# Ids from sorted keys, a split first product, 4096-byte runs and a reordered last unit in a two-layer block kernel

## The reference

```python
scores = jax.nn.sigmoid((xt @ router_w).astype(jnp.float32))
biased = (scores + router_b).reshape(T, N_GROUPS, EXPERTS_PER_GROUP)   # 4 groups of 4 experts
group_score = lax.top_k(biased, 2)[0].sum(-1)
best_group = jnp.argmax(group_score, axis=-1)
local = lax.top_k(in_group, 2)[1]                                      # 2 experts of the best group
gate = take(scores, expert_idx); gate = gate / gate.sum(-1, keepdims=True)
...
def expert_block(args):
    xi, e = args
    return (jax.nn.silu(xi @ w_gate[e]) * (xi @ w_up[e])) @ w_down[e]   # 1024 -> 256 -> 1024
...
x = layer_norm(DEEPNORM_ALPHA * x + ffn, ln2_g[layer], ln2_b[layer])
```

## Time and profile before

| | us |
|---|---|
| median of 3 runs (1299.04 to 1300.09) | 1299.23 |
| the profiled execution, its own time | 1301.88 |
| its span, first to last instruction | 1300.1 |
| PE busy (share of the span) | 1236.1 (95%) |
| DVE busy | 837.8 (64%) |
| ACT busy | 633.7 (49%) |
| queue of DMAs issued by SP, share of 16 engines | 58.4% |

### The profile page before, as it was taken

How to read it: one execution, slowest core, us unless ns; L and a number is a source line. 1 busy time by engine, 2 the same in 40 slices (tenths; PEclk the granted TensorE clock), 3 DMA queues, 4 the chain that set the end, 5 groups by cost and what they waited for, 6 DMA issues and landing times.

```text
span 1300.1 us, 17517 instructions
## 1 busy us (share of the span) xinstructions
PE 1236.1 (95%) x7044; PEld 665.3 (51%) x7048; DVE 837.8 (64%) x1060; ACT 633.7 (49%) x705; POOL 93.6 (7%) x60
## 2 busy tenths in 40 slices
PE   7999999999999999999999998999989979899996
PEld 4676565446654444656657753433345655343333
DVE  6687776988774477555567757433786676743376
ACT  4467565445553264444456634433644584343361
POOL 1000000000000014000005200011002100001100
PEclk9999999999999999999999998999999999899999
DMA  9474444655655565656652015699954600669990
GB/s 316 147 250 160 156 130 140 224 199 189 226 195 194 195 213 186 218 202 214 198 194 66 2 66 187 226 320 369 381 200 164 225 32 33 198 222 322 368 376 35
DMA packets 152812, 258.09 MB, mean 199 GB/s; under 512 B 8913, under 2 KB 81692, under 8 KB 152732
## 3 DMA queue, kind: packets, MB, share of 16 engines
q1 hardware_dynamic: 152732, 256.98, 58.4%
HBM read 255.88 MB, written 1.07 MB: 198 GB/s over the span
## 4 chain that ended last, share of the span: by engine, by line
PE 77%; DVE 8%; DMA 5%; SPq 3%; ACT 3%; issue 2%; DVEq 1%; POOL 1%; POOLq 0%; ACTq 0%
PE ps L1108 12%; PE ps L821 10%; PE ps L1375 9%; PE ps L1152 6%; PE ps L1110 6%; PE ps L802 6%; PE ps L1068 3%; PE ps L1420 3%; PE ps L839 3%; PE ps L1358 2%; DVE w_ring L2082 2%; DMA w_ring<-in_exp_w_up 2%; PE ps L1479 2%; DMA w_ring<-in_exp_w_down 2%; PE ps L1295 2%
## 5 line engine op out<-in xcount | busy, mean ns | idle before, releaser
L2082 DVE SCALAR_TENSOR_TENSOR w_ring<-w_ring,w_hi 128x2048 f16<-128x2048 f32 (+3 forms) x155 | 345.9, 2240 | 120.4 <-ACT w_hi L1636 119.6
L1636 ACT ACTIVATE w_hi<-w_ring 128x2048 f16<-128x2048 f32 (+3 forms) x155 | 285.6, 1851 | 185.8 <-PE ps L1152 50.9
L1108 PE MATMUL ps<-actT,w_hi 128*128 128x512 f16 x608 | 197.8, 379 | 0.0
L1110 PE MATMUL ps<-actT,w_ring 128*128 128x256 f16 x608 | 165.7, 273 | 0.0
L1636 ACT ACTIVATE arena<-ps 128x256 f16<-128x256 f32 (+8 forms) x97 | 66.1, 695 | 115.5 <-PE ps L1110 74.7
L802 PE MATMUL ps<-w_hi,actT 128*128 128x512 f16 (+2 forms) x384 | 111.8, 367 | 2.8 <-DVE actT L2087 2.8
L821 PE MATMUL ps<-w_hi,actT 128*128 128x512 f16 x352 | 108.4, 383 | 2.9 <-DVE w_ring L2082 2.9
L1108 PEld LDWEIGHTS ps<-actT,w_hi 128*128 128x128 f16 x608 | 59.5, 98 | 71.5
L1375 PE MATMUL ps<-arena 128*128 128x512 f16 x224 | 67.9, 396 | 7.7 <-DVE w_ring L2082 5.1
L821 PE MATMUL ps<-w_ring,actT 128*128 128x512 f16 x192 | 73.4, 382 | 0.0
L802 PE MATMUL ps<-w_ring,actT 128*128 128x512 f16 (+2 forms) x192 | 70.5, 367 | 0.0
(11 more groups left out here) (462 smaller groups left out, 2205.1 us busy)
## 6 DMA issues: line engine op xcount, KB each, us to landing
w_ring<-in_dil_w_in SPq DMA_DIRECT2D x36, 1024.0 KB, 5.2
w_ring<-in_w_ff SPq DMA_DIRECT2D x32, 1024.0 KB, 5.1
w_ring<-in_w_in SPq DMA_DIRECT2D x24, 1024.0 KB, 5.1
w_ring<-in_exp_w_gate SPq DMA_DIRECT2D x48, 512.0 KB, 8.7
w_ring<-in_exp_w_up SPq DMA_DIRECT2D x48, 512.0 KB, 8.7
w_ring<-in_exp_w_down SPq DMA_DIRECT2D x20, 1024.0 KB, 10.5
w_ring<-in_sb_w_in SPq DMA_DIRECT2D x12, 1024.0 KB, 5.9
arena<-in_exp_w_down SPq DMA_DIRECT2D x10, 1024.0 KB, 9.9
```

Source lines behind the costliest of these rows:

```text
L1108: pe.matmul(ps[:, bank + c, :], w_h[:, k, cols], aT[:, kk, :], start=(kk == 0), stop=False, skip_group_check=True)
L1110: ins = pe.matmul(ps[:, bank + c, 0:S], w_l[:, k, cols], aT[:, kk, 0:S], start=False, stop=(kk == KD - 1), skip_group_check=True)
L1636: return act.activation(dst, src, ACT.Copy, scale=scale)
L2082: dve.scalar_tensor_tensor(out=lo16(h)[:, 0:kn * c], in0=slot(h)[:, 0:kn * c], scalar=W_POW, in1=hi16(h)[:, 0:kn * c], op0=ALU.mult, op1=A ...
```

## The change

- `expert_ids`: two keys (counts ascending and descending), the eight largest of each by `dve.max`, their positions by `dve.max_index` straight into `expert_at` (now unsigned, counted from 0, SP adds 1). The copy of the counts and the permutation (two comparisons over 7 and 8 ranks) come after the ids are signalled.
- Expert gate and up weights are loaded with `(p k)` in place of `(k p)`: a partition takes rows 8p to 8p + 7, so four rows of 256 f32 are one run of 4096 bytes. In SBUF a half then holds gate as one piece and up as another, and the matmul's moving operand is 2 x 256 columns out of two pieces (`gate_and_up`). To match, the router's weights are loaded with `(p k)`, and the stationary operands that bring the activations into this order are taken with a step of 8 elements: in `turn_tile` of turns 5 and 7 (f32) and in `gather` (f16).
- PE's start: `up(0)`'s first half, `router(0)`, `turn_tile(turn, 1)`, `up(0)`'s second half, `router(1)`, `up(1)`. Six idle matmuls stand before `down(0)` and four after `down(1)`.
- PE's end: the loop stops before the last unit. Then `turn_h(14)`, `tokens(12)`, `down(13)`, `down(14)`, wait for `y_low(13)`, `token_tile(13, 0)` (this completes tile 0), `up(15)`, `token_tile(13, 1)`, `turn_h(15)`, in layer 0 `turn_tile(6, 0)`, and `last_down(15)`. After it 6 idle matmuls in place of 8. DVE does the norm of tile 0 before `weigh(15)`. `RELEASES`, ACT's and DVE's orders follow.

```diff
@@ RELEASES
-    RELEASES += up_halves(_i) if _i < NU and UNITS[_i][1] != 0 else []
-    RELEASES += down_halves(_i - 2) if _i >= 4 and UNITS[_i - 2][1] != 0 else []
+    _up = up_halves(_i) if _i < NU and UNITS[_i][1] != 0 else []
+    _down = down_halves(_i - 2) if _i >= 4 and UNITS[_i - 2][1] != 0 else []
+    RELEASES += _down + _up if _i == NU - 1 else _up + _down
@@ SP, loads
-            sp.dma_start(router_w[:, :, :], a["router_w_2"].rearrange("(k p) e -> p k e", p=P)).then_inc(sig("ld_router"), 16)
+            sp.dma_start(router_w[:, :, :], a["router_w_2"].rearrange("(p k) e -> p k e", p=P)).then_inc(sig("ld_router"), 16)
-                wg = a["exp_w_gate_2"][layer].rearrange("e (k p) n -> p e k n", p=P)
-                wu = a["exp_w_up_2"][layer].rearrange("e (k p) n -> p e k n", p=P)
+                wg = a["exp_w_gate_2"][layer].rearrange("e (p k) n -> p e k n", p=P)
+                wu = a["exp_w_up_2"][layer].rearrange("e (p k) n -> p e k n", p=P)
-                        expert[r] = sp.value_load(expert_at[0:1, r - 1:r], min_val=1, max_val=NE - 1)
+                        c = r if raw(r) else r - 1
+                        expert[r] = sp.value_load(expert_at[0:1, c:c + 1], min_val=0, max_val=NE - 2) + 1
-                    dst = place(h).rearrange("p (o k) n -> p o k n", o=1)
-                    for c, w in ((slice(0, DE), wg), (slice(DE, 2 * DE), wu)):
-                        sp.dma_start(dst[:, :, :, c], w[:, bass.ds(expert[r], 1), 4 * b:4 * b + 4, :])\
+                    dst = slot(h).rearrange("p (o a k n) -> p o a k n", o=1, a=2, k=4)
+                    for c, w in enumerate((wg, wu)):
+                        sp.dma_start(dst[:, :, c, :, :], w[:, bass.ds(expert[r], 1), 4 * b:4 * b + 4, :])\
@@ PE
+                    c = slice(k, D, KD) if i in (5, 7) else slice(k * P, (k + 1) * P)
-                                       x_norm[:, t, k * P:(k + 1) * P], ident)
+                                       x_norm[:, t, c], ident)
+                def gate_and_up(v, k):
+                    return v.rearrange("p k n -> p (k n)").rearrange("p (a k n) -> p k a n", a=2, k=4)[:, k, :, :]
-                                ins = pe.matmul(ps[:, bank, :], x[:, kk, c], w[:, k, :], start=(kk + m == 0),
+                                ins = pe.matmul(ps[:, bank, :], x[:, kk, c], gate_and_up(w, k), start=(kk + m == 0),
-                    k, c = slice(P * (f % 8), P * (f % 8) + P), slice(512, D) if f < 8 else slice(0, 512)
+                    k, c = slice(f % 8, D, KD), slice(512, D) if f < 8 else slice(0, 512)
-                up(0)
-                turn_tile(turn, 1)
+                up(0, (0,))
                 pe.wait_ge(sig("ld_router"), 16)
                 router(0)
+                turn_tile(turn, 1)
+                up(0, (1,))
                 pe.wait_ge(sig("xp_act"), 4 * turn + 4)
...
+                idle_turns(6, 0)
                 down(0)
                 down(1)
+                idle_turns(4, 6)
                 fills((0, 1))
-                for i in range(2, NU):
+                for i in range(2, NU - 1):
...
-                turn_h(NU - 1)
+                turn_h(NU - 2)
+                tokens(NU - 4)
+                down(NU - 3)
                 down(NU - 2)
                 pe.wait_ge(sig("moe_y_lo"), len(FEW) * (layer + 1))
                 token_tile(NU - 3, 0, True)
+                up(NU - 1)
                 token_tile(NU - 3, 1)
+                turn_h(NU - 1)
+                if layer == 0:
+                    turn_tile(6, 0)
                 last_down(NU - 1)
-            turn_tile(6, 0)
-            idle_turns(8, 4)
+            idle_turns(6, 4)
@@ DVE, expert_ids
-                    dve.scalar_tensor_tensor(out=r_key, in0=ps[:, 7, 0:n], scalar=1.0 * NE, in1=row_tie, op0=ALU.mult, op1=ALU.add)
+                    for i in range(2):
+                        dve.scalar_tensor_tensor(out=r_key[:, i, :], in0=ps[:, 7, 0:n], scalar=(1.0, -1.0)[i] * NE,
+                                                 in1=row_tie[:, i, :], op0=ALU.mult, op1=ALU.add)
+                    dve.drain()
+                    for i in range(2):
+                        dve.max(r_sorted[:, i, :], r_key[:, i, :])
+                    dve.drain()
+                    for i in range(2):
+                        ins = dve.max_index(expert_at[:, 8 * i:8 * i + 8], r_sorted[:, i, :], r_key[:, i, :])
+                    ins.then_inc(sig("route_dve"), 1)
                     dve.tensor_copy(r_cnt[:, NE:3 * NE - 1], ps[:, 7, NE:3 * NE - 1])
+                    for i, k in enumerate((slice(0, 7), slice(7, n))):
+                        rows = [P, 7 + i, n]
+                        dve.tensor_tensor(r_perm[:, k, :], r_key[:, i:i + 1, :].broadcast_to(rows),
+                                          r_sorted[:, i, 0:7 + i].unsqueeze(2).broadcast_to(rows), ALU.is_equal)
                     dve.drain()
-                    dve.tensor_tensor(r_gt, r_key.unsqueeze(1).broadcast_to([P, n, n]), r_key.unsqueeze(2).broadcast_to([P, n, n]),
-                                      ALU.is_gt)
-                    dve.drain()
-                    dve.tensor_reduce(r_order, r_gt, AX.X, ALU.add)
-                    dve.drain()
-                    dve.tensor_tensor(r_perm, r_order.unsqueeze(1).broadcast_to([P, n, n]),
-                                      row_rank.unsqueeze(2).broadcast_to([P, n, n]), ALU.is_equal)
-                    dve.drain()
-                    dve.tensor_tensor(r_gt, r_perm, row_id.unsqueeze(1).broadcast_to([P, n, n]), ALU.mult)
-                    dve.drain()
-                    dve.tensor_reduce(r_id, r_gt, AX.X, ALU.add)
-                    dve.drain()
-                    dve.tensor_copy(expert_at[:, :], r_id).then_inc(sig("route_dve"), 1)
@@ DVE, end of the experts
-                for i in range(2, NU):
+                for i in range(2, NU - 1):
...
+                y_low(NU - 3)
+                dve.wait_ge(sig("x_full"), m + 2)
+                for h in range(2):
+                    dve.wait_ge(sig("first_tile"), (7, 12)[layer] + h)
+                    norm_half(0, h)
+                norm_sums(0)
+                if layer == 0:
+                    scale_tile(7, 0, bn_mv[:, 0, 0:1])
+                else:
+                    last_gain(0)
+                weigh(NU - 1)
                 h_low(NU - 1)
```

More of the change, by code:

```diff
@@ L23 @@
 I32 = mybir.dt.int32
+U32 = mybir.dt.uint32
 ALU = mybir.AluOpType
@@ L259, in constants @@
     e = np.arange(1, NE)
-    rows = np.concatenate([inv, earlier, NE - 1 - e, e - 1, e]).reshape(1, 77).repeat(P, 0).astype(f)
+    rows = np.concatenate([inv, earlier, NE - 1 - e, 16 * S + e]).reshape(1, 62).repeat(P, 0).astype(f)
     return {"c_mats": mats, "c_band": band.astype(f), "c_onehot": onehot,
@@ L286, in build @@
         mats = sb("mats", [P, 10, P])
-        crow = sb("crow", [P, 77])
+        crow = sb("crow", [P, 62])
         brow = sb("brow", [P, 24 + NE])
@@ L371, in build @@
         pos_i = sb("pos_i", [P, T], I32)
-        expert_at = sb("expert_at", [P, NE - 1], I32)
+        expert_at = sb("expert_at", [P, NE], U32)
         router_w = sb("router_w", [P, KD, NE])
@@ L468, in build @@
         r_cnt = take(3 * NE)
-        r_key, r_order, r_id = (take(NE - 1) for _ in range(3))
+        r_key = take(2 * (NE - 1)).rearrange("p (a e) -> p a e", a=2)
+        r_sorted = take(NE).rearrange("p (a k) -> p a k", a=2)
         r_perm = take((NE - 1) ** 2).rearrange("p (k e) -> p k e", e=NE - 1)
@@ L1341, in hidden_ready, with up @@
                         pe.wait_ge(sig("moe_hT"), singles_before(NU) * layer + singles_before(i) + 1)
-                def up(i):
+                def up(i, part=(0, 1)):
                     ranks, t = UNITS[i]
@@ L1358, in up @@
                                     ins = pe.matmul(ps[64 * j:64 * j + 64, bank, :], xg_f[:, kk, c + 64 * j:c + 64 * j + 64],
-                                                    w[j][:, k, :], start=(kk == 0), stop=(kk == KD - 1), skip_group_check=True)
+                                                    gate_and_up(w[j], k), start=(kk == 0), stop=(kk == KD - 1),
+                                                    skip_group_check=True)
                                     if k == 3:
@@ L1368, in up @@
                         u, c = (aT_hi, aT_lo), slice(P * t, P * t + P)
-                    for b in range(2):
+                    for b in part:
                         h = 2 * n0 + EXPERT_AT["up", ranks[0], b]
@@ L2008, in experts @@
                 splits(1)
-                for i in range(2, NU):
+                for i in range(2, NU - 1):
                     splits(SPLIT_EARLY.get(i, 0))
-                    if i == NU - 1 and layer == 0:
-                        hi(2 * SBI0)
                     silu(i)
@@ L2018, in experts @@
                     splits(SPLIT_LATE.get(i, 0))
-                    if i == NU - 1 and layer == 0:
-                        hi(2 * SBI0 + 1)
```

(44 more changed lines are left out.)

5 lines of the change are left out of this document (1 added, 4 removed).

## The result

The changed kernel takes 1286.8 us (median of 4 runs, 1285.4 to 1289.3) where the kernel before took 1299.7 in the same runs. The ratio is 0.9899, 95% interval 0.9886 to 0.9912: 13.1 us faster, 11.4 to 14.8. The profiled execution took 1287.27 us with a span of 1285.5, 14.6 us less than the span of before. The forecast was 1282.3, so the gain was overestimated by about 4 us; the time lies inside the range.

The account below looks back on a forecast made before the run. It took waits on a full DMA queue, plus half clock behind idle gaps, to hold back a PE busy 95% of the span. 5.6 + 11.0 + 3.9 - 1.7 - 1.9 = 16.9 us, so 1299.2 to 1282.3, range 1273 to 1293.

Parts of the forecast that it names:

- Start: Start of the experts, both layers: earlier keys, ids and first landing move up(2) by 2.8 us per layer, bounds 0.4 to 3.6.
- so 0.4 us less: First pair of id-dependent loads: 1 MiB takes 2.6 us at 402 GB/s instead of 3.0 at 351.
- Middle: Long middle of each layer's experts: 4096-byte runs speed the full queue, gaining 5.5 us a layer, bounds 0 to 6.1.
- One sign on the list of what would show the prediction right: Middle of either layer: no gap over 1 us before split weights.
- What PE could use: Middle, per layer: gaps of 2.56, 0.98 and 0.73 us plus 1.85 of half clock, 6.1 us, the most PE could gain.
- End of layer 0: From the end of down(12) to the second mixer's projections and their first 24 matmuls: gain 3.9 us, bounds 0 to 6.2.
- T: The end of down(12), from which the ends of the layers are counted: 947.8 us in layer 0, 1272.1 in layer 1.
- the list of what would show it: Signs of a right forecast; here, the second mixer's projections start 22 us after down(12).
- End of layer 1: Last products of layer 1: the new wait and unit 15's steps lose 1.7 us, bounds +1 and -3.5.
- One fall of the clock: Behind the new 2.3 us wait before tokens(12): one fall to half clock, 1.85 us, charged for the two layers.
- Strided operands: Step-8 stationary operands in gather and turn_tile, and the two-piece moving operand: cost taken as 0.
- Rival 2: Slow strided loads: gather's weight loads pass 216 ns, at 353 ns using up the gain; 1300 to 1317 us; chance 0.09.

Follow-up runs that it names:

- after_alone: Changed kernel, but SP waits until rank 1's first pair has landed before issuing the next: 1292.4 us, ratio 0.9930.
- only_runs: Kernel before with only the 4096-byte runs and the strided stationary and two-piece moving operands that go with them: 1290.7 us, ratio 0.9924.
- after: The changed kernel itself, with all parts of the diff, against the kernel before: 1286.8 us, ratio 0.9899.
- after_oldend1: Changed kernel with the old order at the end of layer 1 only, up(15) directly behind down(12): 1284.0 us, ratio 0.9868.
- better: Changed kernel with up(15) split around tokens(12) and token_tile(13, 0), weigh(15) before tile 0's scaling, last_tile(0) before the wait for last_down: 1281.1 us, ratio 0.9856.
- better_idle: The version better with ten more idle matmuls directly before up(2): 1282.2 us, ratio 0.9859.
- after_1k: Changed kernel with each weight half taking every second row, so runs of 1024 bytes; strides and orders kept: 1297.5 us, ratio 0.9976.
- better_order: The version better with three roundings of w_down halves and their remainders moved behind y_high and y_low: 1280.3 us, ratio 0.9842.
- only_tail: Kernel before with only the new end of the experts, in both layers: 1299.9 us, ratio 0.9992.
- only_ids: Kernel before with only the new expert_ids and SP's reading of expert_at: 1298.3 us, ratio 0.9982.
- only_head: Kernel before with only PE's new start order and the six and four idle matmuls: 1297.4 us, ratio 0.9968.

## Why the prediction was nearly right, and what it missed

**Direction and main cause: right.** Run length was named as the largest term and is: 9.9 us alone, 10.0 taken away. The queue rate was predicted at 402 GB/s and is 410. By the Trainium skill, "DMA: Bandwidth & Descriptors", Specifications (a limit of about 358 GB/s for one core, which is half of the rate of a stack that two cores share), only about 2 us of it would have come, by the prediction's estimate. Here one core runs the kernel, and the trace disagrees, with 410 GB/s over 10 us.

**Start: predicted 2.8 a layer, measured 2.3 and 2.2.** The earlier keys (0.9 us, 0.85 predicted), `up(1)` at full clock (5.35 us) and the ids (1.25 predicted, 1.03 measured) came: the first load was issued 2.7 us earlier in layer 1 and 3.1 in layer 0, 2.4 predicted. The step that failed is the first landing, "so 0.4 us less": it took 0.56 us more in layer 1 and 0.80 in layer 0. I had divided 1 MiB by the rate of a full queue, but this landing does not follow that rate: sharing with the loads behind costs 0.8 us, as after_alone shows, and the rest stays open. The bounds of the term held.

**Middle: predicted 5.5 a layer, measured 3.7 and 3.8.** This is the term that was mis-sized, by 3.5 us over both layers, the largest miss. One sign on the list of what would show the prediction right failed with it: a gap over 1 us (1.72, before `up(10)`) stays before split weights in layer 0. What PE could use was right (2.56 + 1.85 + 0.98 + 0.73 = 6.1), and the low clock went. But 2.3 us of gaps stay in layer 1 (0.82 + 0.86 + 0.61) and about 2.6 in layer 0, and 6.1 less these is nearly what came. Two things stand behind it. First, I counted the lead of the start and that of the queue as separate gains. With long runs but the old start, only_runs had 4.6 and 5.1 us here, 0.9 and 1.4 more than the changed kernel. The four traces with the changed kernel's start and long runs (after, after_oldend1, better and better_idle) take 101.2 to 102.3 us for the middle of layer 0 and 100.7 to 101.4 for that of layer 1, only_runs 100.5 and 100.0. That PE arrives there with a lead, finds the queue still full and gives part of the lead back is my reading of it; with short runs (after_1k) only 0.65 and 0.07 us were given back, so the reason is not shown. Second, the queue behind an instruction: `y_high` and `y_low` stand behind the rounding of a `w_down` half that now ends the wait. better_order took the second away and these gaps went.

**End of layer 0: predicted 3.9, measured 3.8.** The wait before `tokens(12)` was 2.16 us (2.3 predicted), the projections started at T + 22.2, as the list of what would show it says, and their first 24 matmuls took 5.34 us. The 1.85 us that the prediction charges for 24 matmuls at half clock is too much: 7.03 us is their time behind an idle gap, 5.18 that in a running stream. Behind a gap they take 5.34, so a fall costs 1.7.

**End of layer 1: predicted -1.7, measured -1.9.** The old end is better there, as after_oldend1 shows.

**One fall of the clock, 1.85 us: it did not come.** Behind the 2.16 us wait the clock fell in none of the two places of the changed kernel. It did at one of two places in after_1k (950.0 us), at the one that after_oldend1 has (943.5), at both of after_alone (944.3 and 1265.1) and at none of only_tail: 4 times of 9. These traces do not show what decides it, and the term is a mean of 0 to 3.7. What the prediction did not see is the half clock at `up(2)` of layer 0 (0.66 in the stretch above): the four idle matmuls after `down(1)` still leave a gap of 3.0 us. It was free, as better_idle shows.

**Strided operands: 0 taken, 0 found.** The loads of `gather` went from 98 to 145 ns and stayed under the 216 ns matmul; those of `turn_tile` from 140 to 156 ns on the mean of all, strided or not; the eight strided products of one `turn_tile` took 1.04 us in only_runs, as those without a step did before. Rival 2 needed 353 ns. The Trainium skill, "SBUF — State Buffer", Door 1, sees `gather` at the edge of the free steps, and its loads did become slower here: 98 ns in each of the four kernels without the step (before, only_ids, only_head, only_tail), 144 or 145 in only_runs, after_1k and the changed kernel. That the step is the cause is shown, that its lines are is not.

**Sum.** Predicted 5.6 + 11.0 + 3.9 - 1.7 - 1.9 = 16.9. Measured between the two traces 4.5 + 7.5 + 3.8 - 1.9 = 13.9, and 0.7 from outside; between the medians 13.1. The clock fall that did not come made up for half of what the middle lacked; that part of the agreement is luck.

## What to carry to other kernels

When a stretch is bound by a full DMA queue, first look at the packet size of what fills it: here a layout that makes each partition's run four times as long was worth 10 us, and the other three parts 3.1 on top of it (7.5 as the sum of each alone). Gains of parts measured alone need not add: here 4.3 us of 17.4 were missing, half ahead of the full stretch and half in it. And the half clock at `up(2)` cost nothing, since the next operand was not ready: look at what the engine waits for after the slow stretch before covering a gap with idle work.

## What was not expected of the hardware

- One core read 410 GB/s over 10 us with 4096-byte runs, and 333 to 380 over stretches of 10 us from 1180 us on in after_1k, where only the `w_down` halves have them.
- The first 1 MiB pair, alone in the queue, took 5.3 us from its second issue in both layers; shared, five times 5.03 to 5.06 with short runs and fourteen times 5.6 to 6.3 with long ones, but also 5.29, 5.44, 5.59, 5.57 and 6.76 with short runs (the last two in after_1k). What sets it stays open.
- Behind idle gaps of the same 2.16 us the clock fell 4 times of 9; at `up(2)` it fell behind gaps of 2.70, 2.92 and 3.00 us and not behind 2.81 (layer 1 of the changed kernel) and 2.83 (layer 0 of better_order).
- f16 weight loads with a step of 8 elements took 145 ns instead of 98.
